# Gate and up weights laid out with 16 neighbouring rows of d on a partition

## The reference

```
hdn = silu(xblk @ w_gate[e]) * (xblk @ w_up[e])     # w_gate, w_up: (32, 2048, 512)
yb  = hdn @ w_down[e]                               # w_down: (32, 512, 2048)
y   = segment_sum(yb * row_w[:, None], row_tok)
```

## Time and profile before

| what | value |
|---|---|
| median of three runs | 2403.87 us |
| span of the profiled execution | 2400.7 us |
| TensorE busy | 2126.0 us, 89% |
| VectorE busy | 1226.9 us, 51% |
| ScalarE busy | 615.4 us, 26% |
| matmuls of line 1827 (gate and up) | 546.3 us |
| matmuls of line 1809 (transposes of xb) | 124.3 us |
| DMA moved | 513.14 MB in 267282 packets |

### The profile page before, as it was taken

The page is one execution under the profiler, slowest core; times in us unless marked ns, Lnnn a source line. Parts: engine busy times, 40 slices in busy tenths (PEclk is TensorE's granted clock), DMA queues, the critical chain, the costliest instruction groups (busy, mean ns, idle before and its releaser), DMA issues.

```text
span 2400.7 us, 28280 instructions
## 1 busy us (share of the span) xinstructions
PE 2126.0 (89%) x10294; PEld 1279.7 (53%) x10294; DVE 1226.9 (51%) x1866; ACT 615.4 (26%) x915; POOL 358.4 (15%) x131
## 2 busy tenths in 40 slices
PE   3999999899998886996399999999999999999992
PEld 3787778777876665885333333333433333333331
DVE  6766655765563554014234444444444444444447
ACT  4223322333233444112212212212212212212211
POOL 2323222222223211443200000000000000000002
PEclk9999999999999996998699999999999999999995
DMA  5512121211122112424599999999999999999961
GB/s 174 158 53 70 45 58 37 70 52 52 44 68 68 45 46 98 140 91 173 166 337 370 371 361 363 376 345 366 380 358 361 363 359 361 376 361 360 384 221 71
DMA packets 267282, 513.14 MB, mean 214 GB/s; under 512 B 13456, under 2 KB 105808, under 8 KB 245488
## 3 DMA queue, kind: packets, MB, share of 16 engines
q1 hardware_dynamic: 263648, 491.53, 57.2%
q0 software_dynamic: 3024, 16.95, 3.3%
q10 hardware_dynamic: 576, 4.19, 0.4%
HBM read 499.92 MB, written 12.72 MB: 214 GB/s over the span
## 4 chain that ended last, share of the span: by engine, by line
PE 74%; DVE 16%; issue 5%; ACT 3%; DMA 1%; DVEq 0%; POOL 0%; SPq 0%; ACTq 0%; POOLq 0%
PE bank L1827 22%; PE bank L1853 10%; PE bank L1500 7%; PE bank L1800 6%; PE bank L1502 6%; PE bank L1501 6%; PE bank L1809 5%; PE bank L1632 2%; PE bank L1629 2%; PE bank L1621 2%; DVE half L1053 2%; PE bank L1839 1%; DVE gd_L L1174 1%; DVE hid L1437 1%; DVE sc L1226 1%
## 5 line engine op out<-in xcount | busy, mean ns | idle before, releaser
L1827 PE MATMUL bank<-wpiece,xbT 128*64 128x512 f32 x2048 | 546.3, 643 | 19.5 <-DVE xbT L1418 18.6
L1411 DVE TENSOR_TENSOR r<-r,bank 128x512 f32<-128x512 f32 x512 | 343.5, 686 | 304.4 <-PE bank L1800 302.4
L534 POOL TENSOR_TENSOR wlo<-raw,whi 128x2048 fp32r<-128x2048 f32 x61 | 284.2, 4660 | 698.7 <-ACT whi L659 472.4
L1500 PE MATMUL bank<-hTh,wlo 128*128 128x512 f32 x720 | 307.6, 427 | 19.1 <-POOL wlo L534 14.3
L1502 PE MATMUL bank<-hTh,whi 128*128 128x512 f32 x720 | 284.5, 395 | 0.0
L1501 PE MATMUL bank<-hTl,whi 128*128 128x512 f32 x720 | 284.1, 395 | 0.0
L1800 PEld LDWEIGHTS bank<-yhl,place 128*128 128x128 f32 x512 | 92.3, 190 | 300.2 <-DVE r L1411 243.2
L1827 PEld LDWEIGHTS bank<-wpiece,xbT 128*64 128x64 f32 x2048 | 125.1, 143 | 226.8 <-issue 226.8
L1800 PE MATMUL bank<-yhl,place 128*128 128x512 f32 x512 | 234.9, 489 | 9.9 <-DVE r L1411 9.9
L1853 PE MATMUL bank<-wpiece,hidT 128*64 128x512 f32 x1024 | 232.1, 606 | 0.5 <-ACT hidT L916 0.5
L926 ACT ACTIVATE yw<-bank,slot_tw 64x512 f32<-64x512 f32 x256 | 174.7, 682 | 154.5 <-PE bank L1853 151.2
(11 more groups left out here) (302 smaller groups left out, 2362.2 us busy)
## 6 DMA issues: line engine op xcount, KB each, us to landing
wpiece<-in_w_gate SPq DMA_DIRECT2D x128, 1024.0 KB, 6.9
wpiece<-in_w_up SPq DMA_DIRECT2D x128, 1024.0 KB, 9.1
wpiece<-in_w_down SPq DMA_DIRECT2D x128, 1024.0 KB, 7.4
raw<-in_w_in SPq DMA_DIRECT2D x45, 1024.0 KB, 5.6
raw<-in_w_o SPq DMA_DIRECT2D x16, 1024.0 KB, 5.0
xt<-in_x SPq DMA_DIRECT2D x4, 1024.0 KB, 9.2
h_scr<-xt SPq DMA_DIRECT2D x4, 1024.0 KB, 4.4
r<-h_scr SPq DMA_DIRECT2D x1, 4096.0 KB, 13.5
```

The costliest lines, as they stand in the source:

```text
L534: pool.tensor_tensor(wlo[sl][:, :, :].rearrange("p k n -> p (k n)"), raw[sl][:, :], whi[sl][:, :, :].rearrange("p k n -> p (k n)").bitcast ...
L1411: dve.tensor_tensor(v, v, [BS, BO][c % 2][:, :], ALU.add).then_inc(comb_done, 1)
L1500: mm(bank, lo_, rh, start=first, stop=False)
L1827: i = mm(B0[SLOTS * h:SLOTS * (h + 1), :], xbT[:, c, :], wpiece[2 * kg_ + h][:, k * F:(k + 1) * F], start=c == 0, stop=c == KD - 1)
```

## The change

The view of w_gate and w_up puts the 16 neighbouring rows 16 p to 16 p + 15 on partition p in place of the rows p, p + 128 and so on. A piece (4 of the 16 steps) is then, on each partition, 4 neighbouring rows, 8 KB in one run, in place of 4 runs of 2 KB. To match, step c of the transposes takes the columns c, c + 16, c + 32 and so on of xb. The weights of down, the buffers, the order and the semaphores stay.

```
-    gate_v = w_gate[0].rearrange("e (k p) f -> p e k f", p=P)
-    up_v = w_up[0].rearrange("e (k p) f -> p e k f", p=P)
+    gate_v = w_gate[0].rearrange("e (p k) f -> p e k f", p=P)
+    up_v = w_up[0].rearrange("e (p k) f -> p e k f", p=P)
...
+            xbv = xb[:, :].rearrange("s (p k) -> s k p", k=KD)
+
             def block_pe(t):
...
                     for k in range(8):
-                        i = mm(PA[g][:, k * SLOTS:(k + 1) * SLOTS], xb[:, (8 * g + k) * P:(8 * g + k + 1) * P],
+                        i = mm(PA[g][:, k * SLOTS:(k + 1) * SLOTS], xbv[:, 8 * g + k, :],
                                cst[0:SLOTS, 0:SLOTS], start=True, stop=True)
```

## The result

| | kernel before | changed kernel |
|---|---|---|
| median of the runs | 2404.37 us (4 runs) | 2556.51 us (4 runs, 2551.4 to 2559.6) |
| span of the profiled execution | 2400.7 us | 2557.9 us |
| mean granted clock | 0.939 | 0.892 |

The ratio is 1.0632, with a 95% interval of 1.0614 to 1.0650. The forecast was 2404 us, the range ended at 2480, and rival A at 2528.

A forecast was written before the change was run, and what follows sets the result against it. The prediction took TensorE to bound the expert stage, with the DMA paced by it. It summed 0 for the pieces and 0 for the transposes on a 2400.7 us span, median 2403.87, to 2404 us; range 2396 to 2480.

The forecast's parts named there:

- rival A: Transposes: every strided column costs a full access, load pace doubles to about 221 ns; 2511, up to 2528 us; chance 0.17.
- The bound: Expert stage: TensorE never waits for a DMA there, and SyncE, which issues the weight transfers, waits for TensorE.
- Part 1: Gate and up pieces: 8 KB runs, fewer packets, landings of 7.4 us hidden by TensorE's work; cost and gain 0.
- Part 2: Transposes reading xb columns 64 bytes apart: no instruction added, 32 instructions keep 3.73 us a block; cost 0.
- slack of a factor two per element: Transposes: moving data enters at 0.45 ns an element, the weight load takes 0.9, so the stride would not show.
- The step before it: Transposes: the weight load sets the pace at about 0.9 ns a column, and nothing hides a slower one.
- two readings of the Trainium skill: Transposes: first, a new 16-byte line at each access is penalised; second, loads at half the moving rate might just absorb it.
- The upper bound: Transposes: at most 221 ns an instruction, the slowest pace seen for this load, 104 ns more, 107 us in all.
- 10 x 1.7 = 17 us: Gate/up matmuls: a longer quiet stretch before them could add low clock to the ten blocks that have none.
- Rival B: Transposes: loads no longer overlap, 188 ns each, 73 us more, 2477 us; anything from 5 us up counts; chance 0.22.
- C: TensorE's clock: a new rhythm of DMA or loads ends low-clock events, at most 36 us faster, 2368 us; chance 0.08.

The follow-up runs named there:

- layout_only: The kernel before with only the weight layout changed to 8 KB runs, transposes still reading neighbouring columns of xb: 2405.76 us, ratio 1.0004.
- near2: The changed kernel with 2 neighbouring rows on a partition in place of 16, columns of xb 8 bytes apart, 4 KB runs: 2406.67 us.
- near4: The changed kernel with 4 neighbouring rows on a partition in place of 16, columns of xb 16 bytes apart, 8 KB runs: 2554.83 us.
- twice: The kernel before with each transpose of xb done two times, neighbouring columns, same result: 2671.08 us, ratio 1.1081.
- tmode_near: The kernel before with 15 of the 16 transposes of a block in TensorE's transpose mode, neighbouring columns: 2445.26 us, ratio 1.0182.
- early_tmode: The kernel before with 15 of 16 transposes in transpose mode and the next block's xbT copied before the last two quarters of yw and yhl: 2340.66 us.
- near8: The changed kernel with 8 neighbouring rows on a partition in place of 16, columns of xb 32 bytes apart, 8 KB runs: 2557.32 us.
- split_far: The changed kernel with one of the two combines after the transposes placed after each group of 8 transposes: 2555.00 us, ratio 1.0634 to the kernel before.
- inter_near: The kernel before with the next block's transposes three at a time between the groups of down matmuls and xbT copied earlier: 2557.32 us, ratio 1.0619.

## Why the prediction was wrong, by its steps

**The bound** was read rightly: TensorE, and a DMA paced by it. layout_only is the proof.

**Part 1, the pieces**, held: 168979 packets, no wait for a wpiece, cost and gain 0. Its price for a landing, 7.4 us, was too high (4.8 measured), which the cover made harmless.

**Part 2, the transposes, is the step that failed.** The 32 instructions took 7.14 us in place of 3.73, 106 us over 31 blocks where the sum had 0, and the low clock that came with it took 45 more. "I take 0" rested on "half the rate at which the same memory feeds the same engine" and "slack of a factor two per element". The moving operand that gave the 0.45 ns an element reads neighbours, four to a 16-byte line. It shows how fast elements come, not how fast new lines come, and says nothing of slack in the second. near2 and near4 put the edge where two elements share a line: 3.92 and 7.65 us. The step before it, that the load sets the pace and nothing hides a slower one, was right, and made the error cost its full amount in every block. Of the two readings of the Trainium skill, I followed the second, with columns / 1.2 ns; near4 decides for the first.

**The upper bound** of that step, 221 ns, came from a load slowed by the clock, another cause than the one at work. That it fits the number (223 measured, 106 us of 107 forecast under A) is luck: with columns 16 and 32 bytes apart a load takes 239 and 244 ns, above the bound.

**Rival A's price** was short in its second term, "10 x 1.7 = 17 us". The ten blocks without low clock did get it (13 by the chain's count), but low clock also came in the down matmuls of every second block, 1.6 us each, and lasted longer at gate/up. 45 us measured. I had counted the events of one place and not asked what else a longer stretch would slow.

**Rival B** (188 ns) and C had nothing in them. A got 0.17, and the range was cut below it.

Shown by runs: the whole loss follows the columns; the step lies between 8 and 16 bytes; the low clock appears without stride when the stretch is longer (twice), appears with short transposes when TensorE idles (tmode_near), and goes when the way to gate/up is short (early_tmode). Left open: why alternate blocks differ, why near8 and split_far pay less low clock than the changed kernel though their way is as long or longer, why 64 bytes costs 0.5 us a block less than 16 and 32, and why the strided load costs 223 ns as a plain fp32 matmul and 125 in transpose mode.

## What to carry to other kernels

Before a layout is changed for longer DMA runs, look whether any engine waits for a DMA; where TensorE bounds and the DMA has time to spare, the run length is worth nothing, and the stride that it puts into an operand on the chain is paid in full. Keep at least two float32 columns of a stationary operand in each 16 bytes (tried here with loads of 128 columns from 64 partitions). Where a matmul group is cut short or moved, count the low clock anew: it moved into other groups in inter_near and made up the whole loss of tmode_near. Where a short instruction group on the critical engine is made quicker, look what other engines do meanwhile: here the time moved only after the copies were taken out from behind them, 2445 to 2341 us.

## What the runs showed of the hardware

- A float32 weight load of 128 columns follows TensorE's clock when two or four columns share 16 bytes (117 to 123 ns at 2.4 GHz, 221 at 1.2), and takes about 223 to 244 ns at either clock when each has its own 16 bytes.
- In transpose mode a load keeps the load port busy 73 ns with neighbouring columns and 125 ns with columns 64 bytes apart.
- Small transposes put between pairs of 512-column down matmuls cost 135 ns each in place of 117 and also slow the down matmuls (1.01 us for four in place of 0.88). Once the clock is low there, it can stay so for the whole group (0.53 over 21.9 us).
- The granted clock can fall while TensorE is never idle: in twice from 1.00 to 0.55 in the midst of its quick transposes.
- At the same pace of TensorE, 8 KB runs landed gate pieces in 6.4 us median in place of 6.9 (layout_only).
